# Mixers of a hybrid encoder step: the convolution and the forget gate of the next unit between a unit's state update and its norm

## The chip, the cores and the metric

The kernel runs on one core of one Trainium2 chip. The metric is the device time of one execution in microseconds (us). The kernel before took 3684.36 us, the median of 3 runs (3683.18 to 3689.75). The profile is of one further execution, which took 3678.0 us; its span from the first to the last instruction is 3676.2 us.

Engines are named as in the profile: PE is TensorE (matmuls and transposes), PEld its weight loads, DVE is VectorE, ACT is ScalarE, POOL is GpSimd, SP is SyncE, which issues the DMAs of this stage.

## The reference, cut to what matters

One layer runs over 1024 prompt tokens and 8 x 16 sample tokens (1152 in all) of width 1024. Two mixers stand side by side, each 512 wide, and the kernel handles them together in four units of 128 channels.

```python
# head group A: HGRN2, one head of 128 channels for each unit, chunks of 64 tokens
f = lb + (1.0 - lb) * sigmoid(zf);  k = 1.0 - f;  logf = log(f);  q = silu(zq);  v = zi
cum = cumsum(logf within a chunk)
qd = q * exp(cum);  kd = k * exp(-cum)
att = where(mask, qd @ kd.T, 0)
o = att @ v + qd @ S
S = exp(last)[..., None] * S + (k * exp(last - cum)).T @ v
oA = rmsnorm(o, g_hgrn_norm) * silu(zg)
# head group B: width-4 causal convolution, then RG-LRU, 128 channels for each unit
xc = conv_b + sum(xp[:, j:j + L] * conv_w[j] for j in range(4))
r = sigmoid(xc @ w_a + b_a);  i = sigmoid(xc @ w_x + b_x)
log_a = -8 * r * softplus(-lam);  a = exp(log_a)
b = sqrt(-expm1(2.0 * log_a)) * (i * xc)
h = scan(a, b);  oB = h * gelu(zy)
```

Behind the mixers come an output projection, a retrieval of experts (PEER), an embedding gate and a last norm, none of which is touched.

## The kernel before, in words

The stages of the kernel run one after the other, each in a block that ends in a barrier of all engines. An input projection writes z, transposed to channels x tokens, to a scratch in DRAM. `mixers` (lines 427 to 856) reads it back, works through four units, and leaves its result in the tile `cat`. The output projection then starts.

`mixers` has two blocks. In the first (lines 528 to 560), SP issues the loads of unit 0 and POOL fills constants. In the second, every engine runs the same loop of four passes in its own written order, and semaphores tie the engines together. No scheduler moves anything: the order in the text is the order on the engine. What a unit does, with the lines:

- PE transposes the old convolution and RG-LRU states (L797) and v (L800), multiplies the convolved x with the two gate weights (L807, six matmuls into six PSUM banks), forms the attention scores (L814), transposes the decayed keys (L819), forms the state increments (L825, L830), and forms the output o of all nine token tiles (L838 to L845). At the end it transposes two small results (L849, L852).
- DVE copies the unit's parameters (L671) and the old state (L676), begins the convolution (L677, L679), finishes the forget gate f (L683) and k = 1 - f (L686), adds the three other taps of the convolution (L689, L691, three times), scans log f (L700), prepares q, k and the gates (L704 to L724), masks the attention (L728), updates the 16 prompt states and 8 sample states (L746, L756), scans RG-LRU (L766), and copies the last columns (L767 to L770). After the square of o it takes the mean, the reciprocal root and the normed o (L773 to L777), and writes the two results into `cat` (L780, L786). L786 signals `all_used`.
- ACT waits for `all_used` of the unit before, then computes three sigmoids (L624 to L628), copies v transposed (L630), takes the logarithm (L632), exponentials (L634 to L638), the two gates (L642), Tanh, Exp and Sqrt (L646 to L650), the square of o (L652), the root (L654) and Gelu (L656).
- SP loads a tensor of the next unit as soon as its only buffer is free: v after L800, f and g after L719, q after o is done (L598), x after the last columns are copied (L601), y after Gelu (L603).

The helper `link` on DVE makes each instruction wait for the one before it (L666 to L668).

Of the kernel before, what the change touches and what calls it, by code (L numbers as in the profile page):

```python
# [25 lines left out]
ALU = mybir.AluOpType  # L26
ACT = mybir.ActivationFunctionType
AX = mybir.AxisListType
# [398 lines left out]
def mixers(P, z_dram, cat):  # L427
# [3 lines left out]
    with ExitStack() as ctx:  # L431
# [4 lines left out]
        def s(n):  # L436
# [4 lines left out]
        zq, zf, zv, zg, zy = (sb(n, [128, T]) for n in ("zq", "zf", "zv", "zg", "zy"))  # L441
        xp = sb("xp", [128, SEQ + 3])
        xs = sb("xs", [128, DB, DS + 3])
        sf, sq, cum, e1, e2, e3, xc, r, ig = (sb(n, [128, T]) for n in (
            "sf", "sq", "cum", "e1", "e2", "e3", "xc", "r", "ig"))
        gs = sb("gs", [128, T])
        scan_mask = sb("scan_mask", [128, T])
        vtok, kdtok, att, on = (sb(n, [128, NT, 128]) for n in ("vtok", "kdtok", "att", "on"))
# [14 lines left out]
        cur = sb("cur", [128, NPAR])  # L463
# [15 lines left out]
        def by(x, n):  # L479
            return x.rearrange("p (c n) -> p c n", n=n)  # L480

        consts, in_f, in_q, in_v, in_g, in_y, in_x, in_s, in_rows, in_wg = map(s, (
            "consts", "in_f", "in_q", "in_v", "in_g", "in_y", "in_x", "in_s", "in_rows", "in_wg"))
# [5 lines left out]
        def load_z(e, dst, i, c, sem):  # L489
            e.dma_start(dst[:], z_of(i, c)).then_inc(sem, 16)  # L490

        def load_f(e, i):
            load_z(e, zf, i, 1, in_f)

        def load_q(e, i):
            load_z(e, zq, i, 0, in_q)

        def load_v(e, i):
            load_z(e, zv, i, 2, in_v)

        def load_g(e, i):
            load_z(e, zg, i, 3, in_g)

        def load_y(e, i):
            load_z(e, zy, i, 5, in_y)

        def load_x(e, i):
            e.dma_start(xp[:, 3:], z_of(i, 4)[:, PROMPT]).then_inc(in_x, 16)
            e.dma_start(xs[:, :, 3:], by(z_of(i, 4)[:, SAMPLE], DS)).then_inc(in_x, 16)
# [18 lines left out]
        with nc.Block() as block:  # L528
            @block.sync
            def _(e):  # L530
                for load in (load_f, load_x, load_v, load_q, load_g, load_s, load_y):
                    load(e, 0)


            @block.gpsimd
            def _(e):
                o = Order(e, consts)
                for m, value in ((mask_p, 1.0), (mask_s, 1.0), (bmask, 1.0), (scan_mask, 1.0), (att, 0.0), (qdz, 0.0),
                                 (wg, 0.0), (rows_in, 0.0), (cols_out, 0.0)):
                    o.did(nc.gpsimd.memset(m[:], value))  # L540
                o.did(nc.gpsimd.memset(states[:, 0], 0.0))
                o.did(nc.gpsimd.memset(xp[:, 0:3], 0.0))
# [22 lines left out]
         state_t, xc_ready, silu_g, gates, va_ready, sqrt_b, gelu_y, oc_ready, oc_t, rows_ready, self_ok) = (s(n) for n in (  # L565
# [3 lines left out]
             "state_t", "xc", "silu_g", "gates", "va", "sqrt_b", "gelu_y", "oc", "oc_t", "rows", "self"))  # L569
        NSTORE = 6  # L570

        with nc.Block() as block:
            @block.sync
            def _(e):
                nc.sync.sem_inc(stored, NSTORE * 16)

                def unit(i, more):
# [35 lines left out]
                with e.Fori(0, 3) as i:  # L613
                    unit(i, True)
                unit(3, False)
# [3 lines left out]
            def _(e):  # L619
                f = nc.scalar.activation  # L620
                with e.Fori(0, 4) as i:
                    e.wait_ge(all_used, i + 1)
                    e.wait_ge(in_f, (i + 1) * 16)
                    f(sf[:], zf[:], ACT.Sigmoid).then_inc(sig_f, 1)  # L624
                    e.wait_ge(in_q, (i + 1) * 16)
                    f(sq[:], zq[:], ACT.Sigmoid).then_inc(sig_q, 1)
                    e.wait_ge(in_g, (i + 1) * 16)
                    f(e3[:], zg[:], ACT.Sigmoid).then_inc(sig_g, 1)  # L628
                    e.wait_ge(v_t, i + 1)
                    f(vtok[:], ps_v, ACT.Copy).then_inc(v_tok, 1)  # L630
                    e.wait_ge(f_ready, i + 1)
                    f(cum[:], sf[:], ACT.Ln).then_inc(ln_f, 1)  # L632
# [5 lines left out]
                    f(e3[:], cum[:], ACT.Exp).then_inc(exp_dl, 1)  # L638
                    e.wait_ge(cur_ready, i + 1)
# [16 lines left out]
                    f(sq[:], zy[:], ACT.Gelu_apprx_tanh).then_inc(gelu_y, 1)  # L656

            @block.vector
            def _(e):
                v = nc.vector  # L660
                nc.vector.sem_inc(all_used, 1)
                PER = 40
                with e.Fori(0, 4) as i:
                    o = Order(e, self_ok, PER, i)

                    def link(ins):  # L666
                        o.did(ins)
                        o.settle()  # L668

                    e.wait_ge(all_used, i + 1)  # L670
                    v.tensor_copy(cur[:], par[:, bass.ds(i, 1)].rearrange("p a n -> p (a n)")).then_inc(cur_ready, 1)  # L671
# [3 lines left out]
                    e.wait_ge(in_x, (i + 1) * 32)  # L675
                    link(v.tensor_copy(xs[:, :, 0:3], ps_state[:, 0:24].rearrange("p (b j) -> p b j", j=3)))  # L676
# [21 lines left out]

                    e.wait_ge(ln_f, i + 1)
# [12 lines left out]
                    link(v.tensor_tensor(zq[:], zq[:], sq[:], ALU.mult))  # L712
# [3 lines left out]
                    o.did(v.tensor_tensor(zq[:], zq[:], e1[:], ALU.mult))  # L716
# [22 lines left out]
                    link(v.tensor_tensor(ig[:], ig[:], xc[:], ALU.mult))  # L739
# [21 lines left out]
                    link(v.tensor_tensor(ig[:], ig[:], sf[:], ALU.mult))  # L761
                    first_a, first_b = by(r[:, SAMPLE], DS)[:, :, 0], by(ig[:, SAMPLE], DS)[:, :, 0]
                    link(v.tensor_tensor(e3[:, 0:DB], first_a, ps_state[:, 24:32], ALU.mult))
                    link(v.tensor_tensor(first_b, first_b, e3[:, 0:DB], ALU.add))
                    link(v.memset(first_a, 0.0))
                    link(v.tensor_tensor_scan(xc[:], r[:], ig[:], 0.0, ALU.mult, ALU.add))  # L766
# [4 lines left out]

                    e.wait_ge(o_sq, i + 1)
                    link(v.tensor_reduce(rs[:], cum[:].rearrange("p (t c) -> p t c", c=128), AX.X, ALU.add))  # L773
# [6 lines left out]
                    link(v.tensor_tensor(cat[:, bass.ds(i + 4, 1)].rearrange("p a t -> p (a t)"), xc[:], sq[:],  # L780
# [5 lines left out]
                    v.scalar_tensor_tensor(out=cat[:, bass.ds(i, 1)].rearrange("p a t -> p (a t)"),  # L786
                                           in0=flat[:, 0:T], scalar=cur[:, GN:GN + 1], in1=gs[:],
                                           op0=ALU.mult, op1=ALU.mult).then_inc(all_used, 1)
                    o.close()

            @block.tensor
            def _(e):
                mm, tr = nc.tensor.matmul, nc.tensor.transpose
                with e.Fori(0, 4) as i:
                    e.wait_ge(all_used, i + 1)
                    e.wait_ge(in_rows, (i + 1) * 32)
                    tr(ps_state, rows_in[:], P.ident[:]).then_inc(state_t, 1)  # L797
# [34 lines left out]
                    last.then_inc(dss_ready, 1)  # L832
                    e.wait_ge(st_ready, i + 1)
# [14 lines left out]
                    e.wait_ge(oc_ready, i + 1)  # L848
                    tr(ps_rows, cols_out[:], P.ident[:]).then_inc(oc_t, 1)  # L849
# [1309 lines left out]
```

## Time and profile before

| | |
|---|---|
| median of 3 runs | 3684.36 us (3683.18 to 3689.75) |
| the profiled execution | 3678.0 us, span 3676.2 us |
| PE busy | 3229.0 us, 88% of the span |
| DVE busy | 2729.5 us, 74% |
| ACT busy | 1067.2 us, 29% |
| granted PE clock, mean | 0.944 of full speed |
| stretch of the mixers | from 352 us to 606 us after the span's start |
| in it: PE, DVE, ACT busy | 136.0, 180.7 and 105.0 us of 254 us |
| in it: granted PE clock | 0.66 |
| in it: matmul records of PE | 644 |

The page gives for the whole program the busy time of each engine, a strip of 40 slices, the DMA queues, the chain of work that ended last, the costliest groups of instructions and the DMA issues. The mixers are a small part of it, so their rows come from the timeline of each engine, where one row is one instruction or a run of equal ones. A value of 0.5 of the granted clock is 1.2 GHz, 1.0 is 2.4 GHz.

### The profile page before, as it was taken

What the parts mean: (1) busy time and instruction counts of PE and PEld (TensorE: products, weight loads), DVE (VectorE), ACT (ScalarE), POOL (GpSimd) and SP (SyncE); (2) the same over time, 40 slices, a digit from 0 to 9 for tenths busy, and PEclk for the clock granted to TensorE, in tenths of its full rate; (3) what the DMA queues carried; (4) which work ended last, traced back from release to release, by engine and by line L of the source; (5) the groups of instructions that cost most, each with busy time, mean ns of one, the idle gap of its engine ahead of it and who ended that gap; (6) DMA issues with size and microseconds to landing.
All of it is one profiled execution on the core that took longest, in us unless ns stands there. A gap on an engine that the chain in (4) does not pass through costs nothing. (4 is left out here: it accounts for less than half of the span.)

```text
span 3676.2 us, 52714 instructions
## 1 busy us (share of the span) xinstructions
PE 3229.0 (88%) x17880; PEld 2939.3 (80%) x17880; DVE 2729.5 (74%) x5159; ACT 1067.2 (29%) x1419; POOL 957.1 (26%) x796
## 2 busy tenths in 40 slices
PE   6998556889979999988888887879999999999978
PEld 6998335689879999987877877768888888888878
DVE  3010875368888777779999997749999999999853
ACT  3121433221122222244544441122222222222143
POOL 0000000000001222245555556513333333334300
PEclk9999667889989999999999998989999999999989
DMA  3223221011046656679999999969999999999721
GB/s 111 85 88 110 72 83 52 19 33 39 19 140 186 183 170 197 195 246 336 335 350 342 340 340 351 365 232 353 365 358 361 350 350 342 356 368 352 243 82 52
DMA packets 411349, 822.82 MB, mean 224 GB/s; under 512 B 40704, under 2 KB 262800, under 8 KB 403856
## 3 DMA queue, kind: packets, MB, share of 16 engines
q1 hardware_dynamic: 300688, 419.27, 34.5%
q0 software_dynamic: 110592, 402.70, 32.0%
q8 instruction: 35, 0.57, 0.1%
q14 instruction: 34, 0.28, 0.0%
HBM read 696.74 MB, written 125.12 MB: 224 GB/s over the span
## 5 line engine op out<-in xcount | busy, mean ns | idle before, releaser
L232 PE MATMUL ea_pa<-rest_hi,ea_uhi 128*128 128x384 f32 x2048 | 711.1, 347 | 102.2 <-DVE ea_ulo L1419 101.5
L1137 POOL DMA_INDIRECT h<-in_peer_u,ga_rows x384 | 544.9, 1419 | 811.6 <-DVE ea_acc L1546 590.1
L234 PE MATMUL ea_pa<-rest_hi,ea_ulo 128*128 128x384 f32 x2048 | 700.2, 342 | 0.0
L233 PE MATMUL ea_pa<-rest_lo,ea_uhi 128*128 128x384 f32 x2048 | 699.2, 341 | 0.0
L1137 POOL DMA_INDIRECT eo_ring<-in_peer_v,ga_rows x384 | 405.2, 1055 | 693.8 <-DVE h L1829 628.3
L1829 DVE SCALAR_TENSOR_TENSOR h<-eo_ring,eo_share,h 128x1024 f32<-128x1024 f32 x384 | 490.2, 1277 | 0.3 <-DMA eo_ring<-in_peer_v,ga_rows 0.3
L232 PEld LDWEIGHTS ea_pa<-rest_hi,ea_uhi 128*128 128x128 f32 x2048 | 396.8, 194 | 110.4 <-issue 70.4
L1546 DVE CUSTOM_DVE_ANT_0 h<-h,plain 128x1024 f32<-128x1024 f32 x384 | 453.7, 1217 | 36.2 <-DMA h<-in_peer_u,ga_rows 35.5
L233 PEld LDWEIGHTS ea_pa<-rest_lo,ea_uhi 128*128 128x128 f32 x2048 | 396.5, 194 | 0.0
L234 PEld LDWEIGHTS ea_pa<-rest_hi,ea_ulo 128*128 128x128 f32 x2048 | 395.2, 193 | 0.0
L1765 ACT ACTIVATE eo_phi<-eo_prod 128x512 fp32r<-128x512 f32 x192 | 121.6, 633 | 770.6 <-DVE eo_prod L1803 695.0
L232 PE MATMUL eo_held<-eo_vhi,eo_phi 128*128 128x512 f32 x768 | 299.9, 391 | 21.4 <-DVE eo_vlo L1794 21.4
L1352 ACT ACTIVATE ea_stage<-ea_pa 128x384 f32<-128x384 f32 x256 | 125.8, 492 | 618.7 <-PE ea_pa L234 577.4
L233 PE MATMUL eo_held<-eo_vlo,eo_phi 128*128 128x512 f32 x768 | 299.5, 390 | 0.0
L234 PE MATMUL eo_held<-eo_vhi,eo_plo 128*128 128x512 f32 x768 | 299.5, 390 | 0.0
L232 PE MATMUL eo_part<-eo_vhi,eo_phi 128*128 128x512 f32 x768 | 298.8, 389 | 0.0
L233 PE MATMUL eo_part<-eo_vlo,eo_phi 128*128 128x512 f32 x768 | 298.8, 389 | 0.0
L234 PE MATMUL eo_part<-eo_vhi,eo_plo 128*128 128x512 f32 x768 | 298.8, 389 | 0.0
L1360 ACT ACTIVATE region<-ea_pw 128x512 f32<-128x512 f32 x192 | 201.9, 1165 | 133.5 <-PE ea_pw L1654 81.5
L1794 DVE TENSOR_TENSOR eo_vlo<-region,eo_vhi 128x1024 fp32r<-128x1024 f32 x128 | 156.6, 1224 | 83.3 <-ACT eo_vhi L1760 82.0
L402 DVE TENSOR_TENSOR win_lo<-win_raw,win_hi 128x1024 fp32r<-128x1024 f32 x24 | 29.4, 1226 | 241.9 <-ACT win_hi L375 241.7
L1419 DVE TENSOR_TENSOR ea_ulo<-ea_ut,ea_uhi 128x1024 fp32r<-128x1024 f32 x128 | 156.3, 1221 | 69.0 <-ACT ea_uhi L1346 68.5
(319 smaller groups left out, 6245.4 us busy)
## 6 DMA issues: line engine op xcount, KB each, us to landing
ea_raw<-in_peer_u SPq DMA_DIRECT2D x512, 128.0 KB
region<-in_peer_v SPq DMA_DIRECT2D x128, 512.0 KB
act_scratch<-ea_stage SPq DMA_DIRECT2D x128, 384.0 KB
w_scratch<-region SPq DMA_DIRECT2D x24, 2048.0 KB, 11.1
region<-w_scratch SPq DMA_DIRECT2D x16, 1536.0 KB
region<-act_scratch SPq DMA_DIRECT2D x16, 1536.0 KB
eo_wt<-w_scratch SPq DMA_DIRECT2D x16, 1536.0 KB
eo_at<-act_scratch SPq DMA_DIRECT2D x16, 1536.0 KB
```

The lines of the kernel that those rows point to most:

```text
L232: nc.tensor.matmul(out, w[0], x[0], start=first, stop=False)
L233: nc.tensor.matmul(out, w[0], x[1], start=False, stop=False)
L234: return nc.tensor.matmul(out, w[1], x[0], start=False, stop=last)
L402: nc.vector.tensor_tensor(wlo[:, u], raw[:, u], whi[:, u].bitcast(F32), ALU.subtract).then_inc(lo_done, 1)
L1137: nc.gpsimd.indirect_dma_start(out=dst, out_offset=None, in_=table, in_offset=bass.IndirectOffsetOnAxis(ap=self.rows[:, m % GT, m // GT:m ...
L1352: nc.scalar.activation(stage[:, u, n * ND_W:(n + 1) * ND_W], pa[:, u, n, 0:ND_W], ACT.Gelu_apprx_tanh).then_inc(gelued, 1)
L1360: nc.scalar.activation(dst, pw[:, q % 2], ACT.Copy, scale=1.0 / G_SCALE).then_inc(w_ready, 1)
L1419: nc.vector.tensor_tensor(chunks(ulo[:, r % 2]), ut[:], chunks(uhi[:, r % 2]).bitcast(F32), ALU.subtract).then_inc(lo_done, 1)
L1546: v_.tensor_tensor_reduce(out=ring[r], in0=ring[r], in1=plain[:, m % GT], scale=1.0, scalar=0.0, op0=ALU.mult, op1=ALU.add, accum_out=dst) ...
L1765: nc.scalar.activation(phi[:, t % 3], prod[:, t % 3], ACT.Copy).then_inc(phi_done, 1)
L1794: v.tensor_tensor(vlo[:, u, jj], raw[:, jj % 2], vhi[:, u, jj].bitcast(F32), ALU.subtract).then_inc(vlo_done, 1)
L1829: v.scalar_tensor_tensor(out=h_t, in0=ring[:, m % RING], scalar=share[:, m:m + 1], in1=h_t, op0=ALU.mult, op1=ALU.add).then_inc(gathered, 1)
```

## The change

The loop of four passes becomes straight code with the unit number as a constant. On DVE a unit is split into `head` (parameters, old state, convolution, forget gate), `main` (from the scan of log f to the last columns) and `tail` (from the mean of the squares to `cat`). The head of the next unit is written between `main` and `tail` of the present one. On ACT the sigmoids and the logarithm of the next unit are written between Sqrt and the square of o. On PE the transpose of the next unit's old states moves ahead of the outputs o.

So that both units can be alive, q, the convolution's input and its result, and the parameters get two buffers each. `on` takes over the buffer `kdtok`, the square of o goes to `r` and Gelu to `ig`. The old states are copied once out of PSUM to a new tile `old`. The loads of x and q now run two units ahead: unit 1's are added to the first block.

```diff
+        zq_two, xc_two = sb("zq", [128, 2, T]), sb("xc", [128, 2, T])
+        xp_two, xs_two = sb("xp", [128, 2, SEQ + 3]), sb("xs", [128, 2, DB, DS + 3])
...
+        on = kdtok
...
                 for load in (load_f, load_x, load_v, load_q, load_g, load_s, load_y):
                     load(e, 0)
+                load_x(e, 1)
+                load_q(e, 1)
...
                         e.wait_ge(o_sum, i + 1)
-                        load_q(e, i + 1)
+                        if i + 2 < 4:
+                            load_q(e, i + 2)
                         load_s(e, i + 1)
                         e.wait_ge(oc_ready, i + 1)
-                        load_x(e, i + 1)
+                        if i + 2 < 4:
+                            load_x(e, i + 2)
...
             @block.scalar
             def _(e):
                 f = nc.scalar.activation
-                with e.Fori(0, 4) as i:
-                    e.wait_ge(all_used, i + 1)
+
+                def head(i):
                     e.wait_ge(in_f, (i + 1) * 16)
+                    if i > 0:
+                        e.wait_ge(sf_used, i)
                     f(sf[:], zf[:], ACT.Sigmoid).then_inc(sig_f, 1)
-                    e.wait_ge(in_q, (i + 1) * 16)
-                    f(sq[:], zq[:], ACT.Sigmoid).then_inc(sig_q, 1)
+                    e.wait_ge(in_q[i % 2], (i // 2 + 1) * 16)
+                    f(sq[:], zq_two[:, i % 2], ACT.Sigmoid).then_inc(sig_q, 1)
                     e.wait_ge(in_g, (i + 1) * 16)
+                    if i > 0:
+                        e.wait_ge(e3_used, i)
                     f(e3[:], zg[:], ACT.Sigmoid).then_inc(sig_g, 1)
+                    e.wait_ge(f_ready, i + 1)
+                    f(cum[:], sf[:], ACT.Ln).then_inc(ln_f, 1)
+
+                head(0)
+                for i in range(4):
...
                     f(sf[:], sf[:], ACT.Sqrt).then_inc(sqrt_b, 1)
+                    if i + 1 < 4:
+                        head(i + 1)
                     e.wait_ge(o_sum, i + 1)
-                    f(cum[:].rearrange("p (t c) -> p t c", c=128), ps_o, ACT.Square).then_inc(o_sq, 1)
+                    e.wait_ge(oc_ready, i + 1)
+                    f(r[:].rearrange("p (t c) -> p t c", c=128), ps_o, ACT.Square).then_inc(o_sq, 1)
...
+                head(0)
+                for i in range(4):
+                    main(i)
+                    if i + 1 < 4:
+                        head(i + 1)
+                    tail(i)
...
+                    if i + 1 < 4:
+                        state_rows(i + 1)
                     e.wait_ge(st_ready, i + 1)
...
                     e.wait_ge(oc_ready, i + 1)
+                    e.wait_ge(old_ready, min(i + 2, 4))
                     tr(ps_rows, cols_out[:], P.ident[:]).then_inc(oc_t, 1)
```

The order of the program on DVE around the end of unit 0, before. The first row is the last column copy, and the mean of the squares (L773) follows directly.

```order
L770 COPY mx_cols_out<-mx_xc 128x8
L773 TENSOR_REDUCE mx_rs<-mx_cum 128x9 [waits mx_o_sq]
L71 REGISTER_ALU
L774 TENSOR_SCALAR mx_rs<-mx_rs 128x9 [waits mx_self]
L776 RECIPROCAL mx_rs<-mx_rs 128x9 [waits mx_rms_root]
L71 REGISTER_ALU
L777 TENSOR_TENSOR mx_on<-mx_ps,mx_rs 128x1152 [waits mx_self]
```

The same place after the change. `mx_old` is the new copy of the old states, `mx_xc` the result of the convolution, and L799 is the mean of the squares, L773 before.

```order
L794 COPY mx_cols_out<-mx_xc 128x8
L688 COPY mx_cur<-par 128x12
L693 COPY mx_old<-mx_ps 128x32 [waits mx_in_x1,mx_state_t,mx_cur]
L695 COPY mx_xs<-mx_old 128x8x3 [waits mx_old]
L696 TENSOR_SCALAR mx_xc<-mx_xp,mx_cur 128x1024 [waits mx_self]
L698 TENSOR_SCALAR mx_xc<-mx_xs,mx_cur 128x128 [waits mx_self]
L702 TENSOR_SCALAR mx_sf<-mx_sf,mx_cur 128x1152 [waits mx_sig_f,mx_self]
L705 TENSOR_SCALAR mx_zf<-mx_sf 128x1152 [waits mx_f]
...
L710 SCALAR_TENSOR_TENSOR mx_xc<-mx_xs,mx_cur,mx_xc 128x128 [waits mx_self]
L799 TENSOR_REDUCE mx_rs<-mx_r 128x9 [waits mx_o_sq,mx_xc]
L800 TENSOR_SCALAR mx_rs<-mx_rs 128x9 [waits mx_self]
```

Thirteen instructions of the next unit, from the parameter copy to the last tap, now stand between the two.

The order on ACT from Sqrt to Gelu of unit 0, before.

```order
L650 ACTIVATE mx_sf<-mx_sf 128x1152 [waits mx_va]
L652 ACTIVATE mx_cum<-mx_ps 128x1152 [waits mx_o_sum]
L654 ACTIVATE mx_rs<-mx_rs 128x9 [waits mx_ms]
L656 ACT_TABLE_LOAD
L656 ACTIVATE mx_sq<-mx_zy 128x1152 [waits mx_in_y]
```

The same place after the change. `mx_e` is the tile e3, `mx_f` the semaphore that L702 of DVE signals.

```order
L665 ACTIVATE mx_sf<-mx_sf 128x1152 [waits mx_va]
L632 ACT_TABLE_LOAD [waits mx_sf_used]
L632 ACTIVATE mx_sf<-mx_zf 128x1152 [waits mx_in_f]
L634 ACTIVATE mx_sq<-mx_zq 128x1152 [waits mx_in_q1]
L638 ACTIVATE mx_e<-mx_zg 128x1152 [waits mx_e3_used,mx_in_g]
L640 ACT_TABLE_LOAD
L640 ACTIVATE mx_cum<-mx_sf 128x1152 [waits mx_f]
L670 ACTIVATE mx_r<-mx_ps 128x1152 [waits mx_oc,mx_o_sum]
L672 ACT_TABLE_LOAD
L672 ACTIVATE mx_rs<-mx_rs 128x9 [waits mx_ms]
L674 ACT_TABLE_LOAD
L674 ACTIVATE mx_ig<-mx_zy 128x1152 [waits mx_in_y]
```

Three sigmoids and the logarithm of unit 1 moved ahead of the square of o (L670, L652 before), with two loads of activation tables, and a third such load stands ahead of the root (L672, L654 before).

The order on SP of the loads ahead of unit 0, before.

```order
L490 DMA mx_zq<-z_scratch 128x1152
L490 DMA mx_zg<-z_scratch 128x1152
L512 DMA mx_s<-in_state_hgrn 128x8x128
L490 DMA mx_zy<-z_scratch 128x1152
L528 UNCONDITIONAL_BRANCH
L573 UNCONDITIONAL_BRANCH [waits barrier_Pool_Activation_PE_DVE_SP_release]
L517 DMA mx_rows_in<-in_state_conv 24x128
L519 DMA mx_rows_in<-in_state_rglru 8x128
```

The same place after the change.

```order
L493 DMA mx_zq<-z_scratch 128x1152
L493 DMA mx_zg<-z_scratch 128x1152
L515 DMA mx_s<-in_state_hgrn 128x8x128
L493 DMA mx_zy<-z_scratch 128x1152
L511 DMA mx_xp<-z_scratch 128x1024
L512 DMA mx_xs<-z_scratch 128x8x16
L493 DMA mx_zq<-z_scratch 128x1152
L531 UNCONDITIONAL_BRANCH
L578 UNCONDITIONAL_BRANCH [waits barrier_Pool_Activation_PE_DVE_SP_release]
L520 DMA mx_rows_in<-in_state_conv 24x128
L522 DMA mx_rows_in<-in_state_rglru 8x128
```

Three more transfers stand ahead of the two small ones into `mx_rows_in`.

## Rows read from the trace of the kernel before

**Rows 1.** The waits from 366 to 606 us: waiter, releaser, us, times, longest.

```profile
DVE mx_rs L773 <- ACT mx_cum L652: 36.0, 4, 9.4
```

**Rows 2.** Timeline of DVE, start of unit 1: start us, us, engine, line, operation, idle before.

```profile
424.77 1.40 DVE L786 SCALAR_TENSOR_TENSOR cat<-mx_ps,mx_cur,mx_gs 128x1152 f32 x1
426.31 0.17 DVE L671 COPY mx_cur<-par 128x12 f32 x1
426.99 0.18 DVE L676 COPY mx_xs<-mx_ps 128x24 f32<-128x24 f32 x1 [0.50 <-PE mx_ps L797]
...
428.84 0.88 DVE L683 TENSOR_SCALAR mx_sf<-mx_sf,mx_cur 128x1152 f32<-128x1152 f32 x1 [0.44 <-ACT mx_sf L624]
...
435.28 0.35 DVE L691 SCALAR_TENSOR_TENSOR mx_xc<-mx_xs,mx_cur,mx_xc 128x128 f32<-128x128 f32 x1
435.67 2.56 DVE L700 TENSOR_TENSOR_SCAN mx_sf<-mx_scan_mask,mx_cum 128x1152 f32<-128x1152 f32 x1
...
446.21 1.65 DVE L724 TENSOR_SCALAR mx_vmask<-mx_vtok,mx_bmask 128x128 f32<-128x128 f32 x8
450.01 1.35 DVE L728 COPY_PREDICATED mx_att<-mx_mask_p,mx_ps 128x1024 f32<-128x1024 int32 x1 [2.15 <-PE mx_ps L814]
```

**Rows 3.** Timeline of DVE in unit 0 between the last columns and the mean.

```profile
409.48 0.16 DVE L770 COPY mx_cols_out<-mx_xc 128x8 f32<-128x8 f32 x1
418.33 1.35 DVE L773 TENSOR_REDUCE mx_rs<-mx_cum 128x9 f32<-128x1152 f32 x1 [8.70 <-ACT mx_cum L652]
```

**Rows 4.** Timeline of ACT in unit 1.

```profile
430.75 1.11 ACT L630 ACTIVATE mx_vtok<-mx_ps 128x1152 f32<-128x1152 f32 x1
...
438.26 1.16 ACT L634 ACTIVATE mx_e<-mx_sf 128x1152 f32<-128x1152 f32 x1 [2.63 <-DVE mx_sf L700]
...
442.44 1.16 ACT L638 ACTIVATE mx_e<-mx_cum 128x1152 f32<-128x1152 f32 x1 [1.97 <-DVE mx_gs L714]
443.62 1.28 ACT L642 ACT_TABLE_LOAD   x1
444.92 1.22 ACT L642 ACTIVATE mx_r<-mx_ps,mx_cur 128x1152 f32<-128x1152 f32 x1
...
478.01 1.13 ACT L652 ACTIVATE mx_cum<-mx_ps 128x1152 f32<-128x1152 f32 x1 [21.36 <-PE mx_ps L845]
480.77 0.21 ACT L654 ACTIVATE mx_rs<-mx_rs 128x9 f32<-128x9 f32 x1 [1.63 <-DVE mx_rs L774]
```

**Rows 5.** Timeline of PE in unit 1.

```profile
426.57 2.13 PE L800 MATMUL mx_ps<-ident,mx_zv 128*128 128x128 f32 x9
435.74 6.28 PE L807 MATMUL mx_ps<-mx_xc,mx_wg 128*128 128x384 f32 x12 [7.04 <-DVE mx_xc L691]
446.28 3.57 PE L814 MATMUL mx_ps<-mx_zq,mx_e 128*128 128x128 f32 x18 [4.26 <-ACT mx_r L642]
```

**Rows 6.** Timeline of PE in unit 2.

```profile
496.33 6.71 PE L807 MATMUL mx_ps<-mx_xc,mx_wg 128*128 128x384 f32 x12 [7.04 <-DVE mx_xc L691]
506.88 2.25 PE L814 MATMUL mx_ps<-mx_zq,mx_e 128*128 128x128 f32 x18 [3.84 <-ACT mx_r L642]
```

**Rows 7.** Timeline of DVE in units 1 and 2.

```profile
485.36 1.40 DVE L786 SCALAR_TENSOR_TENSOR cat<-mx_ps,mx_cur,mx_gs 128x1152 f32 x1
...
509.28 1.33 DVE L728 COPY_PREDICATED mx_att<-mx_mask_p,mx_ps 128x1024 f32<-128x1024 int32 x1 [0.83 <-PE mx_ps L814]
```

**Rows 8.** Busy by window, gates of unit 1: window, us, PE, PEld, DVE, ACT, POOL, clock, DMA.

```profile
435.70:442.00 6.30, 6.26 (x12) 3.28 (x12) 6.23 (x5) 2.22 (x2) 0.00 (x0) 0.65 0.00 0
```

**Rows 9.** The same view, from the first loads to their last landing.

```profile
354.00:365.20 11.20, 0.00 (x0) 0.00 (x0) 0.17 (x1) 4.55 (x4) 3.60 (x15) 0.50 1.04 358
```

**Rows 10.** Timeline of PE, first instruction of the mixers.

```profile
366.26 0.47 PE L797 MATMUL mx_ps<-ident,mx_rows_in 128*128 128x128 f32 x1 [17.93 <-DMA mx_rows_in<-in_state_rglru]
```

**Rows 11.** Busy by window, the tail of unit 1.

```profile
478.00:486.80 8.80, 2.27 (x10) 1.78 (x9) 6.07 (x7) 3.79 (x4) 0.00 (x0) 0.68 0.88 259
```

**Rows 12.** The page's DMA queues: packets, MB, share of 16 engines.

```profile
q8 instruction: 35, 0.57, 0.1%
```

More of the change, by code:

```diff
@@ L438, in s @@
             return used[-1]
[L441 to L445, printed above, removed]
+        zf, zv, zg, zy = (sb(n, [128, T]) for n in ("zf", "zv", "zg", "zy"))
+        zq_two, xc_two = sb("zq", [128, 2, T]), sb("xc", [128, 2, T])
+        xp_two, xs_two = sb("xp", [128, 2, SEQ + 3]), sb("xs", [128, 2, DB, DS + 3])
+        sf, sq, cum, e1, e2, e3, r, ig = (sb(n, [128, T]) for n in (
+            "sf", "sq", "cum", "e1", "e2", "e3", "r", "ig"))
         gs = sb("gs", [128, T])
         scan_mask = sb("scan_mask", [128, T])
-        vtok, kdtok, att, on = (sb(n, [128, NT, 128]) for n in ("vtok", "kdtok", "att", "on"))
+        vtok, kdtok, att = (sb(n, [128, NT, 128]) for n in ("vtok", "kdtok", "att"))
+        on = kdtok
         states = sb("states", [128, NCH + 1, 128])
@@ L462, in mixers @@
         par = P.channels.par
-        cur = sb("cur", [128, NPAR])
+        cur_two = sb("cur", [128, 2, NPAR])
+        old = sb("old", [128, 2, 32])
         gps = ctx.enter_context(nc.psum_tensor("mx_ps", [128, 8, 512], F32))
@@ L564, in mixers @@
          st_ready, sn_ready, att_sum, att_ready, qdz_ready, o_sum, o_sq, ms_ready, rms_root, on_ready, on_t,
-         state_t, xc_ready, silu_g, gates, va_ready, sqrt_b, gelu_y, oc_ready, oc_t, rows_ready, self_ok) = (s(n) for n in (
+         state_t, old_ready, sf_used, e3_used, xc_ready, silu_g, gates, va_ready, sqrt_b, gelu_y, oc_ready, oc_t, rows_ready, self_ok) = (s(n) for n in (
              "stored", "cur", "used", "sig_f", "sig_q", "sig_g", "sig_r", "sig_i", "f", "ln_f", "cum", "dl",
@@ L568, in mixers @@
              "st", "sn", "att_sum", "att", "qdz", "o_sum", "o_sq", "ms", "rms_root", "on", "on_t",
-             "state_t", "xc", "silu_g", "gates", "va", "sqrt_b", "gelu_y", "oc", "oc_t", "rows", "self"))
+             "state_t", "old", "sf_used", "e3_used", "xc", "silu_g", "gates", "va", "sqrt_b", "gelu_y", "oc", "oc_t", "rows", "self"))
         NSTORE = 6
@@ L612, in _ @@
                 load_wg(e, 0)
-                with e.Fori(0, 3) as i:
-                    unit(i, True)
-                unit(3, False)
+                for i in range(4):
+                    unit(i, i < 3)
                 e.wait_ge(stored, 5 * NSTORE * 16)
@@ L655, in _ @@
                     e.wait_ge(in_y, (i + 1) * 16)
-                    f(sq[:], zy[:], ACT.Gelu_apprx_tanh).then_inc(gelu_y, 1)
+                    f(ig[:], zy[:], ACT.Gelu_apprx_tanh).then_inc(gelu_y, 1)
             @block.vector
@@ L661, in _, with link, head @@
                 nc.vector.sem_inc(all_used, 1)
[L662 to L671, printed above, removed]
+                o = Order(e, self_ok)
+                def link(ins):
+                    o.did(ins)
+                    o.settle()
+                def head(i):
+                    zq, xc, xp, xs, cur = (x[:, i % 2] for x in (zq_two, xc_two, xp_two, xs_two, cur_two))
+                    v.tensor_copy(cur, par[:, i]).then_inc(cur_ready, 1)
                     e.wait_ge(cur_ready, i + 1)
                     e.wait_ge(state_t, i + 1)
-                    e.wait_ge(in_x, (i + 1) * 32)
-                    link(v.tensor_copy(xs[:, :, 0:3], ps_state[:, 0:24].rearrange("p (b j) -> p b j", j=3)))
+                    e.wait_ge(in_x[i % 2], (i // 2 + 1) * 32)
+                    v.tensor_copy(old[:, i % 2], ps_state[:, 0:32]).then_inc(old_ready, 1)
+                    e.wait_ge(old_ready, i + 1)
+                    link(v.tensor_copy(xs[:, :, 0:3], old[:, i % 2, 0:24].rearrange("p (b j) -> p b j", j=3)))
                     link(v.tensor_scalar(xc[:, PROMPT], xp[:, 0:SEQ], cur[:, CW:CW + 1], cur[:, CB:CB + 1],
@@ L697, in _, with main @@
                     e.wait_ge(xc_ready, i + 1)
+                def main(i):
+                    zq, xc, xp, xs, cur = (x[:, i % 2] for x in (zq_two, xc_two, xp_two, xs_two, cur_two))
                     e.wait_ge(ln_f, i + 1)
@@ L760, in _ @@
                     e.wait_ge(sqrt_b, i + 1)
-                    link(v.tensor_tensor(ig[:], ig[:], sf[:], ALU.mult))
+                    v.tensor_tensor(ig[:], ig[:], sf[:], ALU.mult).then_inc(sf_used, 1)
+                    e.wait_ge(sf_used, i + 1)
                     first_a, first_b = by(r[:, SAMPLE], DS)[:, :, 0], by(ig[:, SAMPLE], DS)[:, :, 0]
-                    link(v.tensor_tensor(e3[:, 0:DB], first_a, ps_state[:, 24:32], ALU.mult))
-                    link(v.tensor_tensor(first_b, first_b, e3[:, 0:DB], ALU.add))
+                    link(v.tensor_tensor(e3[:, 0:DB], first_a, old[:, i % 2, 24:32], ALU.mult))
+                    v.tensor_tensor(first_b, first_b, e3[:, 0:DB], ALU.add).then_inc(e3_used, 1)
+                    e.wait_ge(e3_used, i + 1)
                     link(v.memset(first_a, 0.0))
-                    link(v.tensor_tensor_scan(xc[:], r[:], ig[:], 0.0, ALU.mult, ALU.add))
+                    link(v.tensor_tensor_scan(xc, r[:], ig[:], 0.0, ALU.mult, ALU.add))
                     o.did(v.tensor_copy(cols_out[:, 0:3], xp[:, SEQ:SEQ + 3]))
@@ L770, in _, with tail @@
                     v.tensor_copy(cols_out[:, 28:36], by(xc[:, SAMPLE], DS)[:, :, DS - 1]).then_inc(oc_ready, 1)
+                def tail(i):
+                    zq, xc, xp, xs, cur = (x[:, i % 2] for x in (zq_two, xc_two, xp_two, xs_two, cur_two))
                     e.wait_ge(o_sq, i + 1)
-                    link(v.tensor_reduce(rs[:], cum[:].rearrange("p (t c) -> p t c", c=128), AX.X, ALU.add))
+                    link(v.tensor_reduce(rs[:], r[:].rearrange("p (t c) -> p t c", c=128), AX.X, ALU.add))
                     v.tensor_scalar(rs[:], rs[:], 1.0 / 128, EPS, ALU.mult, ALU.add).then_inc(ms_ready, 1)
@@ L785, in _ @@
                     e.wait_ge(stored, (i + 1) * NSTORE * 16)
-                    v.scalar_tensor_tensor(out=cat[:, bass.ds(i, 1)].rearrange("p a t -> p (a t)"),
+                    v.scalar_tensor_tensor(out=cat[:, i],
                                            in0=flat[:, 0:T], scalar=cur[:, GN:GN + 1], in1=gs[:],
                                            op0=ALU.mult, op1=ALU.mult).then_inc(all_used, 1)
-                    o.close()
+                head(0)
+                for i in range(4):
+                    main(i)
+                    if i + 1 < 4:
+                        head(i + 1)
+                    tail(i)
             @block.tensor
@@ L793, in _, with state_rows @@
                 mm, tr = nc.tensor.matmul, nc.tensor.transpose
-                with e.Fori(0, 4) as i:
+                def state_rows(i):
+                    e.wait_ge(in_rows, (i + 1) * 32)
+                    e.wait_ge(all_used, max(i, 1))
+                    tr(ps_state, rows_in[:], P.ident[:]).then_inc(state_t, 1)
+                state_rows(0)
+                for i in range(4):
+                    zq, xc = zq_two[:, i % 2], xc_two[:, i % 2]
                     e.wait_ge(all_used, i + 1)
-                    e.wait_ge(in_rows, (i + 1) * 32)
-                    tr(ps_state, rows_in[:], P.ident[:]).then_inc(state_t, 1)
                     e.wait_ge(in_v, (i + 1) * 16)
```

35 lines of the change are left out of this document (18 added, 17 removed).

## The prediction

> **What bounds the kernel now.** I read the busy strip of the page first, then the busy time by window, then the waits of the mixers, then the timeline of each engine through one unit, since only there can be seen what each engine does while another waits. In the page the reader sees that the mixers are 254 of 3676 us and that no engine is full in them. So no engine bounds this stage: a chain does, which goes to and fro between DVE, PE and ACT.
>
> Two links matter here. Between a unit's last column copies and the mean of the squares DVE stands idle in each of the four units, 36.0 us in all [rows 1], because PE is forming o; the shortest of these gaps is unit 0's [rows 3], from 409.64 to 418.33, that is 8.69 us. And at the start of each unit PE waits 7.04 us for the convolution before it can form the gates [rows 5], since DVE spends the time from 426.31 to 435.63 on the convolution and the forget gate [rows 2]. The change moves the second piece into the first gap. Outside the mixers nothing is edited, and the next stage starts behind a barrier, so what a unit saves should come off the end one for one.
>
> **The gap: does the head fit?** The head took 435.63 - 426.31 = 9.32 us, with two waits inside, 0.50 for the old states from PE and 0.44 for the sigmoid of f [rows 2]. Both fall away in the new place: PE now transposes the states before it forms o, and ACT has its Sqrt done some 20 us before o (it sat idle 21.36 us ahead of the square [rows 4]). The new copy `old` adds one instruction like L676, 0.18 us and a step of 0.04. Head: 9.32 - 0.94 + 0.22 = 8.60 us, against 8.69 in the shortest gap. It fits with nothing to spare; I put its overrun at 0, and at worst at the two waits come back, (9.54 - 8.69) x 3 = 2.6 us.
>
> On ACT the logarithm of the next unit now stands ahead of the square of o, and it waits for DVE's f. That is ready some 2 us into the head (428.84 - 426.31, less the waits), 6 us before o. The added table load ahead of the root starts when the square ends, at 478.01 + 1.13 = 479.14, takes 1.28 us [rows 4] and is over at 480.42; the root started at 480.77 [rows 4], so the wait for the mean covers it. Tail unchanged, cost 0.
>
> In this trace the ACTIVATE behind a table load starts 0.02 us after the load's end: 443.62 + 1.28, then 444.92 [rows 4]. The Trainium skill (ScalarE: Activation LUTs, What ACT_TABLE_LOAD costs) states a drain of some 1.38 us on top, 2.66 us for a switch. By that rule the root would start at 481.80, 1.03 us late in each of three units, and the sum below would be 3.1 us smaller. The trace speaks against it, and I take the row.
>
> **The start of a unit, after.** Let E be the end of L786: 424.77 + 1.40 = 426.17 [rows 2]. Before, the scan of log f started at E + 9.50 and the masking of the attention, L728, at E + 23.84 (450.01). Everything behind L728 keeps its order up to the square of o, so the gain of a unit is how much earlier L728 starts.
> - DVE starts the scan at E + 0.03. From the scan to the end of L724 it needs 447.86 - 435.67 = 12.19 us [rows 2], so it could begin L728 at E + 12.3.
> - PE starts the transposes of v at E + 0.14 (as DVE restarted at 426.31) and needs 2.13 us [rows 5]; ACT copies v in 1.11 us [rows 4], to E + 3.42; PE begins the gates at E + 3.46, where before it waited for the convolution. They take 6.28 us [rows 5]: E + 9.74.
> - ACT meanwhile loads its table (1.28), does two Exps of 1.16 and the third of 1.16 [rows 4], free at E + 8.2. It waits for the gates, loads a table and computes r: 9.78 + 1.28 + 0.02 + 1.22 = E + 12.30. PE starts the attention 0.14 later, as before (446.14 to 446.28), at E + 12.44.
> - From there to L728 it took 450.01 - 446.28 = 3.73 us: E + 16.17.
>
> So the new limit is no longer DVE but the line v, gates, r, attention, and DVE idles 3.9 us. Of the head's 9.5 us unit 1 keeps 23.84 - 16.17 = 7.67. Unit 2 has slower gates and a faster attention: gates 6.71 and 509.28 - 506.88 = 2.40 to L728 [rows 6, 7], so E + 3.46 + 6.71 + 2.70 + 2.40 = 15.27, against 509.28 - 486.76 = 22.52 before: 7.25. Unit 3 reads like unit 1. Sum 7.67 + 7.25 + 7.67 = 22.6 us.
>
> PE's clock is the open term. The gates ran at a granted 0.65 on average [rows 8], part at 1.2 GHz and part at 2.4; they began after PE had stood for 7.04 us [rows 5]. Now they follow the transposes after 1.2 us, and the attention follows after 2.7 instead of 4.26. Wholly at 2.4 GHz the gates would take 6.28 x 0.65 = 4.1 us, then ACT is the limit (E + 8.2, r at 10.76, attention at 10.90, L728 at 13.3), and the three units gain 10.5 + 9.2 + 10.5 = 30.3. Wholly at 1.2 GHz they take 8.2, and unit 2's attention 1.3 more: 22.6 - 5.6 - 1.3 = 15.6. I take the rows' own clocks, which lie between.
>
> **Unit 0.** It has no earlier gap, so its head stays where it was, with 0.22 us for the new copy. And it starts later: PE's first instruction waited for the old states until 366.26 [rows 10], which landed at the end of the first loads, behind a DMA queue that was full at 358 GB/s [rows 9]. Three transfers now stand ahead of them, 576 + 512 + 64 KB = 1.18 MB: 1.18 / 0.358 = 3.3 us later. Bounds: 0, if the states were late for another reason, and 4.0 at the tail's rate of 259 / 0.88 = 294 GB/s [rows 11], where the same kinds of transfer run. I take 3.3, the row of the very stretch. The later loads of x and q are the same bytes at the same points of SP's order; what stands behind them on SP (y, and the small stores) loses nothing.
>
> **Sum.** 22.6 - 3.3 - 0.2 = 19.1 us. The profiled execution would go from 3678.0 to 3658.9. The median of the runs lies 6.4 above that execution, so 3684.4 - 19.1 = 3665.3.
>
> **Rivals.**
> - The head sticks out. Waits inside it come back, the gates run cold, or both: 15.6 - 2.6 - 4.0 - 0.2 = 8.8 us gained, 3676. For it: a margin of 0.1 us [rows 3]. Against: an overrun costs only itself.
> - The gates and the attention run at 2.4 GHz: 30.3 - 3.5 = 26.8 us gained, 3658. For it: PE's shorter pauses. Against: the attention of unit 1, after 4.26 us of pause, took 3.57 us and unit 2's, after 3.84, took 2.25 [rows 5, 6], so the clock turns on small shifts.
> - The pieces pay each other off: the preloads cost more than shown and the line over the gates takes most of the hidden head, under 7.4 us gained: about 3680.
> - Slower, by one mechanism: straight code must be fetched. The page counts 35 instruction transfers in one queue, 0.1% of 16 engines' span [rows 12], so about 1.7 us each. At a tail the DMA engines are busy to 0.88 of 8.8 us [rows 11], so a fetch that stands behind all of it waits up to 7.7 us more, 9.4 in all. If an engine of the chain stood still for it, two would eat the gain and three, one at each tail, make the kernel slower: 3665.3 + 28.2 = 3693.5. Against: four units of PE are only some 650 matmuls, so the fetches are few, and they would have to come late each time. The Trainium skill (Runtime: NRT & Kernel Launch, Instruction fetch mechanics) says that crossing a block is mostly hidden, and that it is the taken branch which stalls; the trace shows no stall at the old loop's branch either, DVE restarted 0.14 us after L786 [rows 2].
>
> **How the numbers follow.** Forecast, 12 to 27 us gained: 0.76. Head sticks out or cold gates, 7.4 to 12 gained: 0.12. Over 27: 0.03. About the same: 0.06. Slower: 0.03. A measurement of this kernel can tell about 0.2%, 7.4 us, from no change; so faster 0.91, same 0.06, slower 0.03. The time is the forecast's, 3665. The range runs from 3656, where all runs at full clock, to 3676, where the head sticks out.
>
> **What would show it.** In the trace after: DVE's idle before the mean shrinks from 8.7 to 9.4 us to under 1; the scan starts right behind L812 (L786 before); PE's gates start 3.5 us after it; DVE idles some 4 us before the masking; unit 1 takes some 53 us from L786 to L786 where it took 60.6 [rows 2, 7]; the first PE instruction comes some 3 us later. The prediction is wrong if ACT's square starts late behind the logarithm, if the root waits for its table, if units 1 to 3 shrink by less than 5 us each, or if an engine stands still with its semaphores long satisfied.

## The result, and the profile after

| | before | after |
|---|---|---|
| median | 3683.77 us (4 runs, 3681.33 to 3689.75) | 3661.38 us (4 runs, 3657.90 to 3664.03) |
| ratio after/before | | 0.9936, 95% interval 0.9919 to 0.9953 |
| profiled execution, span | 3676.2 us | 3656.2 us |
| end of the last unit | 605.99 us | 585.52 us |

The change gained 22.4 us by the medians; 19.1 had been forecast. In the two profiled executions the last unit ends 20.5 us earlier, and what follows takes 3070 us in both.

DVE around the end of unit 0, after, against [rows 3]; columns as in [rows 2]:

```profile
414.13 0.17 DVE L688 COPY mx_cur<-par 128x12 f32<-128x12 f32 x1
...
422.46 0.35 DVE L710 SCALAR_TENSOR_TENSOR mx_xc<-mx_xs,mx_cur,mx_xc 128x128 f32<-128x128 f32 x1
423.69 1.35 DVE L799 TENSOR_REDUCE mx_rs<-mx_r 128x9 f32<-128x1152 f32 x1 [0.88 <-ACT mx_r L670]
...
429.61 1.40 DVE L812 SCALAR_TENSOR_TENSOR cat<-mx_ps,mx_cur,mx_gs 128x1152 f32<-128x1152 f32 x1
430.93 2.54 DVE L722 TENSOR_TENSOR_SCAN mx_sf<-mx_scan_mask,mx_cum 128x1152 f32<-128x1152 f32 x1
...
448.48 1.35 DVE L750 COPY_PREDICATED mx_att<-mx_mask_p,mx_ps 128x1024 f32<-128x1024 int32 x1 [4.91 <-PE mx_ps L851]
```

The head of unit 1 runs from 414.13 to 422.81, 8.68 us, where DVE had stood; 0.88 us of the wait are left. The scan follows L812 at once. But the masking, L750, waits 4.91 us for the attention where L728 waited 2.15 [rows 2]. The other engines there, after, ACT first, against [rows 4]:

```profile
422.46 1.13 ACT L670 ACTIVATE mx_r<-mx_ps 128x1152 f32<-128x1152 f32 x1 [4.37 <-PE mx_ps L884]
423.61 1.28 ACT L672 ACT_TABLE_LOAD   x1
425.29 0.21 ACT L672 ACTIVATE mx_rs<-mx_rs 128x9 f32<-128x9 f32 x1 [0.40 <-DVE mx_rs L800]
...
441.50 1.28 ACT L657 ACT_TABLE_LOAD   x1 [2.50 <-PE mx_ps L844]
```

Then PE, against [rows 5] and [rows 10]:

```profile
370.13 0.48 PE L829 MATMUL mx_ps<-ident,mx_rows_in 128*128 128x128 f32 x1 [21.82 <-DMA mx_rows_in<-in_state_rglru]
...
431.06 2.18 PE L837 MATMUL mx_ps<-ident,mx_zv 128*128 128x128 f32 x9 [1.69 <-DVE cat L812]
434.56 6.84 PE L844 MATMUL mx_ps<-mx_xc,mx_wg 128*128 128x384 f32 x12 [1.31 <-ACT mx_vtok L646]
444.16 4.18 PE L851 MATMUL mx_ps<-mx_zq,mx_e 128*128 128x128 f32 x18 [2.76 <-ACT mx_r L657]
```

The rows show the new limit of a unit's start: v is transposed on PE and copied on ACT, PE forms the gates, ACT computes r, and PE forms the attention, each step waiting for the one before. The next table collects it from the timelines. E is the end of the unit before; for unit 0, which has none before it, the start of PE's first instruction is taken.

| unit | length before, us | length after | E to masking before | E to masking after | gates after | attention after |
|---|---|---|---|---|---|---|
| 0 | 59.91 | 60.88 | 23.46 | 24.04 | 7.17 | 4.18 |
| 1 | 60.59 | 53.53 | 23.84 | 17.47 | 6.84 | 4.18 |
| 2 | 58.67 | 50.26 | 22.52 | 14.38 | 5.68 | 2.24 |
| 3 | 60.56 | 50.72 | 23.64 | 14.85 | 6.14 | 2.25 |

### The profile page after: what moved, and what is told of

Same layout as the page of the kernel before. It is cut to its first block and busy times, and to the rows that moved or that the text cites. A ratio compares the mean times of both kernels' runs of the same rounds, so it can differ in the third digit from the quotient of the medians.

```text
span 3656.2 us, 52408 instructions
## 1 busy us (share of the span) xinstructions
PE 3230.3 (88%) x17880; PEld 2938.9 (80%) x17880; DVE 2732.2 (75%) x5163; ACT 1068.8 (29%) x1422; POOL 959.5 (26%) x796
## 6 DMA issues: line engine op xcount, KB each, us to landing
eo_at<-act_scratch SPq DMA_DIRECT2D x16, 1536.0 KB, 17.5
```

## Experiments

Single executions of the kernel before took 3677.06 to 3694.18 us and its medians 3683.77 to 3686.03, so pieces of a few us are read off the timelines of the mixers, of which there is one for each kernel. The kernels ran in three groups, each with the kernel before beside it, whose median there was 3685.45, 3686.03 and 3685.47 us. The first group is the next four kernels, the second the four after them, both on one chip; the last three kernels ran on another chip. The first load of the mixers, ahead of which nothing is edited, is issued 350.3 to 351.2 us after the span's start on the first chip and 351.8 to 352.2 us after it on the second (352.1 in the two profiles of the result). Microseconds "over" or "below the changed kernel" are taken from its median in the result, 3661.38.

**The head back at the start of its unit.**

```diff
-                head(0)
                 for i in range(4):
+                    head(i)
                     main(i)
-                    if i + 1 < 4:
-                        head(i + 1)
                     tail(i)
```

and the same on ACT and for the states on PE. 

> Straight code, double buffers, preloads and the three tile swaps of the change stay; only the place of the head goes back to the start of its unit on DVE, ACT and PE. Theory (the gain is the head hidden behind the forming of o): DVE idles 8.5 to 9.5 us before the mean of the squares again in all four units, the scan starts some 9.4 us after the end of the unit before, units 1 to 3 take 58.5 to 60 us instead of 53.5, 50.3 and 50.7, and the time is some 24 us over that of the changed kernel, about 3685. Rival (the gain comes from the straight code and the freed buffers, which drop register instructions and let the loads run ahead): it stays within 5 us of the changed kernel, about 3662 to 3666.

Measured: 3683.64 us, ratio to before 0.9991 (0.9982 to 1.0001), so 22 us over the changed kernel. (The profiled execution was the slowest of this kernel's ten, 3692.22 us.) Units of 60.45, 59.74, 59.77 and 60.96 us; the scan starts 9.2 us after E. DVE's gap, in unit 1:

```profile
481.75 1.35 DVE L797 TENSOR_REDUCE mx_rs<-mx_r 128x9 f32<-128x1152 f32 x1 [8.18 <-ACT mx_r L668]
```

The rival falls: the gain is the place of the head. Straight code, second buffers and loads running ahead are together worth nothing that shows. That is a net figure: this kernel also carries the later start that the next run prices at 3.8 us, so small gains may stand against it.

**The preloads behind the old states.**

```diff
                 load_rows(e, 0)
                 load_wg(e, 0)
+                load_x(e, 1)
+                load_q(e, 1)
```

> The three preloads of unit 1 (x in two transfers, q) are issued behind the old states and the gate weights instead of ahead of them. Theory (the states land at the end of a full DMA queue, and the preloads cost 3.9 us at the start): PE's first instruction of the mixers goes from 370.1 back to 366.3 us, the rest is unchanged, 3.9 us less, about 3657.5. Rival (the block in front ends later because of something else, as its barrier): the first instruction stays at about 370 us and the time at 3661.

Measured: 3655.05 us, ratio 0.9909 (0.9893 to 0.9926). PE's first instruction:

```profile
365.34 0.48 PE L829 MATMUL mx_ps<-ident,mx_rows_in 128*128 128x128 f32 x1 [18.07 <-DMA mx_rows_in<-in_state_rglru]
```

The three other kernels of the group, with the preloads ahead, had it at 368.84 to 368.94, 3.5 us later. Counted from the first load, which was issued at 351.09 here and at 350.69 to 350.93 there, the price is 3.8 us. The units themselves did not change (60.81, 53.49, 50.26, 50.71). The median fell by 6.3 us; no row of the mixers explains the rest.

**v transposed early.**

```diff
                     tr(ps_rows, cols_out[:], P.ident[:]).then_inc(oc_t, 1)
+                    if i + 1 < 4:
+                        v_rows(i + 1)
```

> v of the next unit is transposed on PE right behind o and copied on ACT behind Gelu; the normed o is transposed into the banks of o instead of those of v. Theory (a unit's start is now limited by v, gates, r, attention): the gates start at the end of the unit before instead of 3.55 us after it, the masking of the attention comes 13 to 14.8 us after that end instead of 17.5, 14.4 and 14.9, and the three units together lose some 5 us, about 3656. Rival (DVE's own queue or the clock of PE is the limit): the gates start earlier but run colder behind PE's longer pause, the masking moves by under 1 us a unit, about 3659 to 3661.

Measured: 3654.93 us, ratio 0.9905 (0.9889 to 0.9922). Gates and attention of unit 1, whose E is 429.55:

```profile
429.61 6.76 PE L852 MATMUL mx_ps<-mx_xc,mx_wg 128*128 128x384 f32 x12 [1.69 <-DVE cat L817]
440.07 2.25 PE L859 MATMUL mx_ps<-mx_zq,mx_e 128*128 128x128 f32 x18 [3.71 <-ACT mx_r L660]
```

E to masking: 12.92, 14.29, 12.90 instead of 17.47, 14.38, 14.85, so 6.6 us less, 6.0 of them by the earlier start of the attention and the rest by its length. The attention starts at E + 10.52 in all three, though the gates took 6.76, 6.22 and 6.77 us. The limit ahead of it is now DVE's queue from the scan to L741, then ACT's third exponential, a table load and r:

```profile
436.23 1.16 ACT L655 ACTIVATE mx_e<-mx_cum 128x1152 f32<-128x1152 f32 x1 [1.97 <-DVE mx_gs L741]
```

**PE kept busy between v, gates and attention.**

```diff
                     last.then_inc(gates, 1)
+                    turn(14)        # transposes of the identity, result unused; turn(4) behind v
```

> PE does idle transposes of the identity into a bank that nobody uses: 4 between v and the gates, 14 between the gates and the attention, in every unit. They compute nothing. Theory (of the 17.5 us from unit 1's start to the masking some 4 are PE at 1.2 GHz): with the pauses filled the gates go from 6.84, 5.68 and 6.14 us to about 5, the attention to 2.25 in each unit, and the time falls by about 5 us to 3656. Rival (the clock follows something other than these pauses, and the fillers stand in the way): gates and attention keep their lengths, the attention starts up to 0.5 us later, and the time is the same or up to 2 us longer.

Measured: 3650.73 us, ratio 0.9904 (0.9888 to 0.9921).

```profile
430.42 4.55 PE L849 MATMUL mx_ps<-mx_xc,mx_wg 128*128 128x384 f32 x12 [0.46 <-ACT mx_vtok L646]
437.73 2.25 PE L857 MATMUL mx_ps<-mx_zq,mx_e 128*128 128x128 f32 x18 [1.24 <-ACT mx_r L657]
```

Gates 4.55, 4.11 and 4.79 us, the attention 2.25 in every unit, the masking at E + 13.26, 13.07 and 13.50: 10 us less than the changed kernel in the mixers of the profiled runs, 2.9 of them in unit 0. Against the repeat of the changed kernel below, whose attention was fast by itself, it is 6.7 us. The clock is a term as large as v's place.

**The old states first of all.** SP issues them ahead of all other loads of unit 0, and x ahead of f; POOL clears their tile first, and the preloads go last. 

> The old states are loaded ahead of all other tensors of unit 0, x goes ahead of f, and the preloads of unit 1 stand behind everything in the second block. Theory (the mixers begin when the states land, and the engines could start at the block's barrier): PE's first instruction comes at about 360 us instead of 370, the first unit keeps its length of some 61 us, and the time is 8 to 10 us below the changed kernel's 3661, about 3652. Rival (x, v or the gate weights then come last, or the barrier at the block's end holds everything): the first instruction comes at 363 to 366 and the time is 3655 to 3658.

Measured: 3651.31 us, ratio 0.9908 (0.9892 to 0.9925).

```profile
360.64 0.45 PE L830 MATMUL mx_ps<-ident,mx_rows_in 128*128 128x128 f32 x1 [14.10 <-DVEq L680]
```

PE now waits for DVE's first signal behind the barrier, no longer for a DMA. It comes 10.1 us after the first load, where the three kernels with the preloads ahead had 18.0 to 18.2.

**These three together**, with 18 idle transposes ahead of the attention only. 

> Three findings together: old states first, v transposed early, and 18 idle transposes between gates and attention (they compute nothing). If the pieces act on different waits they add: 9 for the start, 6.6 for v, 2 to 3 for the attention at full clock in all units (DVE's own 12.2 us from the scan is then the limit), so 3661 - 18 = about 3643. Rival (they overlap, since each shortens the same line and DVE's queue is the floor): 3648 to 3652.

Measured: 3643.91 us, ratio 0.9892 (0.9875 to 0.9908). By the medians the sum came out. The profile does not bear it out piece by piece: PE's first instruction comes 9.6 us after the first load, which gives some 8.5 us, and the four units together took 208.9 us, no less than the 208.4 with v early alone. The attention was at 3.7 us in units 0, 1 and 3, so the 2 to 3 us forecast for the idle transposes did not show.

**The kernel before, PE kept busy ahead of o.**

```diff
                     last.then_inc(dss_ready, 1)
+                    turn(44)
                     e.wait_ge(st_ready, i + 1)
```

> The kernel before, with 44 idle transposes on PE between the state increments and o, where PE stood idle 6.2 us (they compute nothing). It asks why the gap that the change filled was there. Theory (o takes 14.3 to 15 us because PE enters it cold and stays at 1.2 GHz): o falls to 8 to 9 us, the gap of DVE before the mean from 9 to about 3 us, and the kernel before gains some 20 to 25 us without any move, about 3662. Rival (o is bound by weight loads, by small matmuls or by the clock falling again inside o): o stays at 14 to 15 us and the time at 3685, or slightly above where the fillers delay o.

Measured: 3663.60 us, ratio 0.9946 (0.9930 to 0.9963): 22.4 us below the kernel before in its group, about as much as the whole change, with nothing moved. In the profiled mixers it is somewhat less, 17.5 us where the change has 24.3. DVE's wait in unit 1, against [rows 1]:

```profile
471.81 1.35 DVE L773 TENSOR_REDUCE mx_rs<-mx_cum 128x9 f32<-128x1152 f32 x1 [2.94 <-ACT mx_cum L652]
```

The windows of unit 1, columns as in [rows 8]: in the kernel before, the pause and then o,

```profile
457.00:463.00 6.00, 0.00 (x0) 0.00 (x0) 5.47 (x17) 0.00 (x0) 0.00 (x0) 0.80 0.00 0
463.00:478.00 15.00, 14.89 (x67) 10.30 (x67) 6.73 (x18) 0.00 (x0) 0.00 (x0) 0.51 0.12 39
```

and with the pause filled:

```profile
456.00:462.00 6.00, 6.00 (x48) 5.24 (x46) 5.47 (x17) 0.00 (x0) 0.00 (x0) 1.00 0.00 0
462.00:471.00 9.00, 8.72 (x70) 6.11 (x67) 6.67 (x17) 0.35 (x1) 0.00 (x0) 1.00 0.21 66
```

o took 8.5 to 8.6 us instead of 14.3 to 15 in units 1 to 3, and 12.97 in unit 0. The length of the last pause does not explain unit 0: the fillers ended 1.38 us before o there, and 1.39 us before it in unit 3, which took 8.57. So the gap that the change fills exists for the most part because PE stands still ahead of o and then forms it at 1.2 GHz.

**The same fillers in the changed kernel.** 

> The changed kernel with the same 44 idle transposes ahead of o (they compute nothing). Theory (in units 0 to 2 DVE's own queue from the state update through the next unit's head is now the limit, o the limit only in unit 3): even where o gets shorter, units 0 to 2 gain at most the 0.9, 0 and 0.3 us that DVE idled before the mean, and unit 3 gains what o loses; 3655 if o falls to 8 us, 3661 if it does not. Rival (o is still the limit everywhere): the gain would be as in the kernel before, 20 us or more.

Measured: 3647.28 us, ratio 0.9899 (0.9882 to 0.9915). DVE's idle before the mean is 0 in units 0 to 2, and in unit 3, which has no head to hide, 3.07 instead of 8.83:

```profile
566.55 1.35 DVE L799 TENSOR_REDUCE mx_rs<-mx_r 128x9 f32<-128x1152 f32 x1 [3.07 <-ACT mx_r L670]
```

As the theory has it, o's length no longer counts in units 0 to 2: from the masking to the end they took 35.87, 36.06 and 35.66 us, as without fillers (36.84, 36.06, 35.88), though o fell to 8.57 in two of them. Unit 3 took 30.10 from masking to end instead of 35.87. The time fell further than the 3655 expected. The profile shows two reasons: a start 2.1 us earlier, 1.8 of them ahead of the first load, and a faster clock in unit 1, with gates of 5.50 and an attention of 2.93 us, so that its masking came at E + 14.89 instead of 17.47. The rest stays open.

**The changed kernel again, and two best versions.** 

> The changed kernel itself once more, on the chip of the two kernels that join the findings. Expected: 3658 to 3664, units 1 to 3 of 53.5, 50.3 and 50.7 us in the trace. If the length of unit 1 (attention at 1.2 GHz, 17.5 us from its start to the masking) is chance, it differs from 53.5 by over 1 us here; if it follows from the order of the work, it repeats.

Measured: 3659.71 us, ratio 0.9926 (0.9910 to 0.9943). Units 1 to 3 took 50.77, 51.00 and 51.03 us. Unit 1's attention:

```profile
441.76 2.25 PE L851 MATMUL mx_ps<-mx_zq,mx_e 128*128 128x128 f32 x18 [2.76 <-ACT mx_r L657]
```

It took 4.18 us in three other executions of this order and 2.25 here, behind the same pause of 2.76 us. Those three agree to within 0.1 us in all gates and attentions of units 1 to 3; they are the changed kernel in the result, the run with the preloads behind and the run with the old states first. So the order on PE alone does not settle the clock. Whether the execution or the chip does is not shown: two of the three ran on the first chip, this one on the second, and the chip of the result is not on record.

> Old states first and v early, with idle transposes (they compute nothing) in each pause of PE: 18 between gates and attention, 44 ahead of o, 7 behind the transposes of v, 7 behind those of the normed o. Theory (what is left is DVE's own queue, some 48.5 us a unit, plus o in the last unit, and the clock decides the rest): units of 59, 48.7, 48.7 and 43 us, 9 us below the kernel with the first three findings (3644), about 3635. Rival (the fillers no longer raise the clock when v is early, since the gates follow a colder stretch): attention at 3.7 us in some units and o at 14 us, 3640 to 3644.

Measured: 3644.01 us, ratio 0.9892 (0.9875 to 0.9909): the rival's case, 9 us over the 3635 of the theory. The attention of units 1 to 3 took 2.25, 3.27 and 4.18 us and the last o 13.0 us, for all the fillers.

> Old states first, v at the unit's start as in the changed kernel, and idle transposes (they compute nothing): 4 behind v, 14 behind the gates, 44 ahead of o. Theory: the start gains 9, the gates and the attention 7 to 10 as in the run with those fillers alone, and the last unit's o some 6: 3661 - 24 = about 3637. If the kernel with v early is the better one by 2 us or more, its earlier gates count even with a full clock; if they are within 1 us, the clock alone was the worth of v's place.

Measured: 3642.06 us, ratio 0.9879 (0.9859 to 0.9898), the best median here, 43.4 us below the kernel before on that chip, but 5 us over the 3637 of the theory. Units of 59.52, 49.02, 48.74 and 43.96 us. It is 2 us below the version with v early, no difference that counts. The attention started at E + 10.97, 10.67 and 11.58 here and at E + 10.52 with v early: where the gates run this fast (4.66, 4.11 and 5.27 us), v's place buys 0.2 to 1.1 us a unit.

## Why the prediction was right

- **Does the head fit?** Yes: 8.60 forecast, 8.68 measured. The overrun set to 0 was 0 in units 0 and 2 and 0.4 us in unit 1, where DVE went from the last tap straight into the mean. Moving the head back to its old place cost the whole gain, 22 us.
- **The tail's extra table load** cost nothing. It ended at 424.89 and the root started at 425.29, released by DVE's mean. By the drain that the Trainium skill states (ScalarE: Activation LUTs, What ACT_TABLE_LOAD costs) the root could not have started before 426.27; the trace decides against it here.
- **The start of a unit.** The gates began at E + 3.55 (3.46 forecast), and v, gates, r, attention became the limit as described; moving v and keeping PE busy each shortened it. Up to the masking the three units gained 6.37, 8.14 and 8.79 us, 23.3 against 22.6 forecast; with what came behind it 7.06, 8.41 and 9.84, together 25.3, and 27.0 in the repeat. What was mis-sized is the clock term: I kept the old lengths of gates (6.28, 6.71) and attention (3.57, 2.25) in their units. After, they were 6.84 and 4.18, then 5.68 and 2.24. The masking came at E + 17.47, 14.38 and 14.85 against 16.17, 15.27 and 16.17. In the repeat all three were at 14.8 to 15.2. That the sum up to the masking is off by only 0.7 us is luck in part: unit 1 came 1.3 us later than forecast, and units 2 and 3 earlier by 0.9 and 1.3.
- **Behind the masking** I expected no change; it shrank by 0.3 to 1.1 us a unit. 0.26 us a unit lies in the tail, which took 7.58 us from the mean's start to E in units 1 to 3 before and 7.32 after. The run without the move has 7.32 too, so this part is not the move's; between Gelu's end and the product that waits for it lay 0.30 us in unit 1 before, and 0.04 after. The rest stays open.
- **The start of the mixers.** 3.3 us forecast, 3.9 in the two profiles, 3.8 in the run that moves the preloads, counted from the first load.
- **Unit 0.** 0.2 forecast, 0.97 in the profile and -0.6 in the repeat; the copy is there (0.19 us and a step). The rest goes mostly with the lengths of gates, attention and o: 7.17, 4.18 and 15.04 us in the profile, 5.70, 3.63 and 14.39 in the repeat, 5.79, 3.71 and 14.33 before.
- **The sum.** In the profiles the mixers gave 25.3 - 3.9 - 1.0 = 20.4 us, against 19.1. The 22.4 us of the medians lie 2 us above that, within what medians move.
- **The rivals.** Not one fetch shows: in the mixers every idle stretch of DVE, ACT and PE's matmuls that the waits list has an engine or a DMA that ended it, though the instruction transfers in the first queue rose from 35 to 39. The sum for wholly cold gates has a slip: at 8.2 us they are 1.9, 1.5 and 1.9 us longer, 5.3 together and not 5.6. It also took 3.57 us for unit 1's attention, which took 4.18 at a granted 0.50 after. With both put right that case gives about 14.2 us for the three units, not 15.6. The 27 us case, everything at 2.4 GHz, is what the fillers show to be reachable, not what the pauses gave by themselves.

What the prediction did not see is why the gap was there. It took o's 15 us as given; they came of PE's low clock, and keeping PE busy would have been the other way to about the same gain.

## What to carry to other kernels

Before work is moved into a gap, ask what makes the gap long: here one engine's low clock, which filling its pause cured for about as much as the move. The two do not add in full, since after the move DVE's own queue is the limit in units 0 to 2: in the profiled mixers the move saved 24.3 us, the fillers 17.5, and both together 33.9. And when a unit's first piece is hidden, work out the line of waits through the other engines too: 9.5 us were hidden and 6.4 to 8.8 of them kept at the masking, by how fast that second line ran. Small transfers that release a stage go ahead of large preloads: here the wrong order cost 3.8 us, and the small ones ahead of everything gained 8.

## What the runs showed of the hardware

- PE formed o at a granted 0.51 for 15 us of uninterrupted work, entering it from a pause of 6.2 us; entering it from 44 transposes it kept 1.00 for 9 us, and took 8.5. With a last pause of 1.1 to 1.4 us behind the fillers, o took 8.6 us in some units and 13.0 in others (8.57 after 1.39 us, 12.97 after 1.38, in one execution).
- The same order with the same pause of 2.76 us ahead gave unit 1's attention 4.18 us in three executions and 2.25 in a fourth, on another chip than two of them. A forecast by one execution's clock was uncertain here by about 2 us for such a step.
- DVE's instructions ran as long beside PE's o as alone: 1.28 us for a tap before and after.
